# Head products of the state-space stage: four bursts behind units three to six become two bursts behind units four and six

## What is computed

```python
CB = jnp.einsum('bcqgn,bckgn->bcgqk', Cc, Bc)
Lmat = jnp.exp(jnp.where(mask, diff, -jnp.inf))
y_diag = jnp.einsum('bcgqk,bcgrqk,bckgrp->bcqgrp', CB, Lmat, xdt)
y_off = jnp.einsum('bcqgn,bcgrpn,bcqgr->bcqgrp', Cc, h_starts, jnp.exp(acs))
```

## Time and profile before

| | us |
|---|---|
| median of 3 runs | 1998.27 |
| lowest, highest | 1996.66, 1999.34 |
| the profiled execution | 1996.18 |
| its span, first to last instruction | 1994.4 |

### The profile page before, as it was taken

The page is one execution under the profiler, slowest core; times in us unless marked ns, Lnnn a source line. Parts: engine busy times, 40 slices in busy tenths (PEclk is TensorE's granted clock), DMA queues, the critical chain, the costliest instruction groups (busy, mean ns, idle before and its releaser), DMA issues.

```text
span 1994.4 us, 27925 instructions
## 1 busy us (share of the span) xinstructions
PE 1935.1 (97%) x10573; PEld 1642.1 (82%) x10573; DVE 1212.2 (61%) x1688; ACT 1000.2 (50%) x1465; POOL 100.3 (5%) x117
## 2 busy tenths in 40 slices
PE   5889999999999999999999999999999999999999
PEld 3558888888888888887879998787889999998887
DVE  3335645776557888767776676656555454555554
ACT  5434323344555666654445434466544555656642
POOL 1010000000014324000000000000000000000000
PEclk9999999999999999999999999999999999999999
DMA  9973322357656666758875455444565655555554
GB/s 342 349 240 112 100 71 85 97 167 225 196 160 190 192 174 183 233 176 290 317 241 159 149 149 148 145 119 140 176 192 171 188 160 175 168 164 169 169 185 164
DMA packets 210040, 360.39 MB, mean 181 GB/s; under 512 B 14264, under 2 KB 61776, under 8 KB 209024
## 3 DMA queue, kind: packets, MB, share of 16 engines
q1 hardware_dynamic: 200448, 349.36, 56.4%
q10 hardware_dynamic: 8848, 8.47, 1.9%
q0 software_dynamic: 624, 0.92, 0.2%
HBM read 356.55 MB, written 2.16 MB: 180 GB/s over the span
## 4 chain that ended last, share of the span: by engine, by line
PE 86%; DVE 5%; DMA 4%; ACT 2%; SPq 2%; issue 1%; POOL 1%; ACTq 0%; POOLq 0%; DVEq 0%
PE acc L652 48%; PE acc L639 15%; PE acc L619 10%; DMA raw_first<-in_w_ada 2%; SPq L498 1%; DVE w_lo L1879 1%; PE side L1022 1%; DMA ex_a<-acs_scratch 1%; PE side L897 1%; DVE conv L2046 1%; PE side L714 1%; PE side L792 1%; PE side L889 1%; ACT w_hi L1221 1%; PE side L950 1%
## 5 line engine op out<-in xcount | busy, mean ns | idle before, releaser
L1879 DVE TENSOR_TENSOR w_lo<-raw,w_hi 128x1024 fp32r<-128x1024 f32 (+1 forms) x552 | 674.5, 1228 | 431.0 <-ACT w_hi L1221 424.0
L1221 ACT CAST w_hi<-raw 128x1024 fp32r<-128x1024 f32 (+1 forms) x544 | 559.9, 1034 | 579.7 <-PE acc L652 383.2
L652 PE MATMUL acc<-w_hi,h_hi 128*128 128x512 f32 (+1 forms) x1312 | 525.2, 400 | 5.8 <-DVE w_lo L1879 4.0
L652 PE MATMUL acc<-w_hi,h_lo 128*128 128x512 f32 (+1 forms) x1312 | 509.7, 389 | 0.0
L652 PE MATMUL acc<-w_lo,h_hi 128*128 128x512 f32 (+1 forms) x1312 | 508.3, 387 | 0.0
L652 PEld LDWEIGHTS acc<-w_hi,h_hi 128*128 128x128 f32 x1312 | 247.1, 188 | 58.6 <-issue 6.3
L652 PEld LDWEIGHTS acc<-w_hi,h_lo 128*128 128x128 f32 x1312 | 246.8, 188 | 52.7
L652 PEld LDWEIGHTS acc<-w_lo,h_hi 128*128 128x128 f32 x1312 | 247.5, 189 | 46.6
L639 PE MATMUL acc<-h_hi,w_hi 128*128 128x256 f32 x896 | 258.3, 288 | 6.9 <-DVE w_lo L1879 5.6
L639 PE MATMUL acc<-h_lo,w_hi 128*128 128x256 f32 x896 | 254.4, 284 | 0.0
L639 PE MATMUL acc<-h_hi,w_lo 128*128 128x256 f32 x896 | 254.3, 284 | 0.0
(11 more groups left out here) (398 smaller groups left out, 2047.5 us busy)
## 6 DMA issues: line engine op xcount, KB each, us to landing
raw<-in_w_in SPq DMA_DIRECT2D x184, 512.0 KB, 4.4
raw<-in_w_in_odd SPq DMA_DIRECT2D x128, 512.0 KB, 3.7
raw<-in_w_in_even SPq DMA_DIRECT2D x96, 512.0 KB, 3.7
raw<-in_w_out SPq DMA_DIRECT2D x64, 512.0 KB, 5.4
raw_first<-in_w_ada SPq DMA_DIRECT2D x58, 512.0 KB, 8.8
gate_w<-in_w_ada SPq DMA_DIRECT2D x32, 512.0 KB, 6.5
raw<-in_w_out_even SPq DMA_DIRECT2D x32, 512.0 KB, 4.8
raw<-in_w_out_odd SPq DMA_DIRECT2D x32, 512.0 KB, 3.9
```

What stands on the lines that cost most here:

```text
L652: o = nc.tensor.matmul(ACC[b][:, 0:n], l, r, start=first and kk == 0 and m == 0, stop=last and kk == 1 and m == 2)
L1221: act.copy(WHI[:, u % 4, :, 0:n], RAW[:, u % 4, :, 0:n]).then_inc(hi_ready, 1)
L1879: dve.tensor_tensor(WLO[:, u % 4, :, 0:n], RAW[:, u % 4, :, 0:n], WHI[:, u % 4, :, 0:n].bitcast(F32), ALU.subtract).then_inc(lo_ready, 1)
```

## The change

On PE `ssd_y` of heads 0 and 1 is issued together behind unit 4, and that of heads 2 and 3 together behind unit 6; before, each had a place of its own behind units 3, 4, 5 and 6. On DVE `heads(g, 2)` moves from step 6 to step 7, `heads(g, 3)` from 7 to 8 and `y_sum` from 8 to 10. No instruction of PE, DVE, ACT, POOL or SP is added or removed; ACT, POOL and SP keep their order.

```diff
             def ssd_hooks(g):
-                return {0: lambda: ssd_cb(g), 1: lambda: ssd_off(g, 1), 3: lambda: ssd_y(g, 0), 4: lambda: ssd_y(g, 1),
-                        5: lambda: ssd_y(g, 2), 6: lambda: ssd_y(g, 3)}
+                return {0: lambda: ssd_cb(g), 1: lambda: ssd_off(g, 1), 4: lambda: (ssd_y(g, 0), ssd_y(g, 1)),
+                        6: lambda: (ssd_y(g, 2), ssd_y(g, 3))}
...
             def ssd_mid(g):
                 return {3: lambda: (off_out(g, 0), off_out(g, 1)), 4: H(heads, g, 0), 5: H(heads, g, 1),
-                        6: H(heads, g, 2), 7: H(heads, g, 3), 8: H(y_sum, g)}
+                        7: H(heads, g, 2), 8: H(heads, g, 3), 10: H(y_sum, g)}
```

## The result

The median went from 1997.55 to 2007.69 us, a ratio of 1.0052 with a 95% interval of 1.0040 to 1.0063 (seven runs each). The forecast was 1994.8, with a range of 1992.2 to 1998.9; the time lies above the whole range. The profiled execution of the changed kernel took 2009.64, its span 2007.9; it is compared with the profiled 1996.18 of before.

A forecast was written before the change was run, and what follows sets the result against it. PE was taken to bound the kernel, through its own work and 2.7 us of waits ahead of L880. Waits of 2.7 and merging of 0.8 off a median of 1998.27 gave 1994.8 us, range 1992.2 to 1998.9.

The forecast's parts named there:

- What bounds the kernel: PE, busy 97% of the span; beside its own work, 2.7 us of waits ahead of L880 over seven stretches.
- Part 1, the merging: On PE, bursts of L897 merged into sixteen records save 0.05 us per pair, 16 pairs: 0.8 us.
- Part 2: Unit 4 on PE ends 0.94 us earlier, rows are asked for earlier, waits of L880 go: 2.7 us, bounds 0 and 2.7.
- rival B: Waits of L880 stay because weight loads share bandwidth with the rows; only merging pays: 1997.5 us, chance 0.18.
- The safety: At least one DVE low part falls before POOL's masks: up to 1 us more cover, not counted as gain.
- Part 3: DVE's new order costs nothing: head 3's matrix has 0.65 us to spare, and the slightly later `y_sum` stays hidden.
- Both hide it: POOL's masking until 666.83 and the eviction's wait for unit 7 until 664.9 cover `y_sum` ending near 663.7.
- C: A whole weight load ahead of the rows makes L880 wait in all seven stretches: 2003.8 us, chance 0.07.
- E: Head 3's decay matrix comes late from DVE, PE waits 0.3 us in eight second bursts: 1997.2 us, chance 0.05.

The follow-up runs named there:

- kernel with every stretch at 28.08: The change's PE order with DVE's old order, rows asked for after low part 6, POOL's copies ahead of its masks: 1994.41 against 1997.64 us, ratio 0.9985.
- kernel with few pieces: The changed kernel with row DMAs of groups 1 to 7 filling only 16 of 128 partitions: 2004.58 us in a single execution.

## Why the prediction was wrong, point by point

**What bounds the kernel** was right: the waits of L880, 2.7 us in all, were all there was to gain beside the merging. The kernel with every stretch at 28.08 is 3.3 us of stretches below before; the prediction had 3.5.

**Part 1, the merging,** was right and right in size. A burst of sixteen takes 1.70, and a stretch without waits 28.08 instead of 28.17, which is 0.045 per merged pair where 0.05 was forecast.

**Part 2 failed at "So the chain starts some 0.9 earlier. The wait of 0.82 goes".** The first half holds: 0.97 by the trace. The step from an earlier issue to an earlier landing doesn't. I took 6.96 as the price of the second row DMA wherever it is issued, and it had been read in one order of issue alone: rows and load 10 within 0.01 us, the next load 3.15 behind. With the rows 0.95 ahead of load 10 it takes 8.0, and with load 11 1.13 behind load 10 it takes 9.3 to 9.7. "The bounds are 0 ... and 2.7" was wrong at its lower end for that reason: the rows landed 0.5 to 2.3 us later in their stretch than before (2.5 in the stretch with the lower clock), and nothing in the text excluded it. The list of what each moved step issues was made for ACT and not for SP: that low parts 6 and 7 back to back ask for loads 10 and 11 back to back stood only in rival B, as bandwidth.

The safety that Part 2 counted is real. With the low parts out of POOL's way a pair of masks takes 1.44 and not 3.39. It is why masks that start at +24.1 in the kernel with the sum at step 9 end in a stretch of 28.65, while in the one with PE's table alone masks from +22.7 end in 29.20. The rule of the Trainium skill named there (page "SBUF — State Buffer", practical consequences) agrees also with the kernel with few pieces, where DVE's step with two SBUF inputs took 0.74 for 0.35 beside the masks.

**Part 3 failed at "`y_sum` near 663.7 instead of 663.07" and "Both hide it".** From the stretch's start that is +24.3; it ended at +28.7, 4.4 later. The step assumed that ACT can start the high part of unit 10 once unit 6 ends, so that load 10 has landed. That was true with a load of 4.8 us. With 10.4 ACT stands idle for 6.07, some 4.4 of them behind the end of unit 6:

```profile
668.24 1.05 ACT L1221 CAST w_hi<-raw 128x1024 fp32r<-128x1024 f32 x1 [6.07 <-DMA raw<-in_w_in]
```

Moving `y_sum` from 8 to 10 tied the chain to L880 to a transfer that had been off it. This is the larger part: 8.0 of the 9.4 us go when the sum stands one step earlier.

**The rivals.** B and C named the right meeting, loads of weights with the rows, and gave it 0.25 together; both had the wrong price. They reckoned with shares of bandwidth, at most 1.7 us for one load, and looked only at the rows. C's sign, a wait in all seven stretches, is there, and C came nearest with 2003.8. None of them, nor the sum, had the weight load itself late. E's delay of head 3's matrix didn't come here, but showed in the kernel with few pieces.

**The size in all.** Of 209.27 - 199.90 = 9.4: merging -0.6 (7 x 0.09), the late load through `y_sum` +8.0 (changed kernel less the one with the sum at 9), the rest +2.0: rows that land late against masks that are quicker, and the one stretch of 30.43, which has most of it. About 1.6 us of the whole is the clock: behind the wait of 2.35 us at 673.42 the granted clock stood at 0.54 for 3.58 us, and PE's busy time in that stretch is 29.99 instead of 28.35. Behind the longest wait, 2.51 us at 735.45, it stayed at 1.00, so the wait alone doesn't explain it. In the kernel with the sum at 9 no stretch shows that, so these 1.6 are in the 8.0.

```profile
673.42:677.00 3.58, 3.58 (x9) 2.93 (x10) 1.91 (x1) 1.55 (x3) 3.14 (x4) 0.54 0.53 158
```

**What stays open.** Why a load that is asked for just behind the rows' many pieces is hardly served for 3 us, with the DMA engines mostly idle, these runs don't settle. The Trainium skill, page "DMA: Bandwidth & Descriptors", section "Queues, rings and completion order", has SP's and ACT's queues as rings of the same engines, each engine taking turns between those with work. By that rule the load would be expected to begin beside the rows at once; the trace shows 80 and 22 GB/s instead in the 3.40 us behind its issue, and 19 packets of weights against 245 of rows. That points to something ahead of the engines' turns, but no run here shows what. The number of pieces matters, and the bytes matter in some groups; more than that isn't shown.

In the kernel before, three L880 wait on `grp_bc`. In two of these three stretches the masks start at +22.7, and in the third at +22.1. A stretch with masks at +22.65 and no wait shows what else counts: POOL's copies take 0.40 each there, and 0.86 in group 2, where DVE multiplies by the gate at the same time (L2210):

```profile
638.55 0.40 POOL L2738 COPY grp_bc<-bT 128x256 f32 x1
...
666.21 2.02 DVE L2210 TENSOR_TENSOR t<-t,gate_tmp 128x512 f32 x2
```

Why the rows land at +22.6 in some groups and at +22.0 in others is open.

## What to carry to other kernels

Before counting an earlier issue as an earlier arrival, list for every DMA queue what is issued within some 2 us around it after the change, and take the flight time from rows with that order; where no row has that order, the lower bound is a loss. When a step moves behind another on an in-order engine, follow that other step's inputs down to their DMA, and ask what happens if this is 5 us late (as load 10 was here). And a consumer that is last (L880) should not stand behind work it doesn't need (the masks): this reordering was worth more than the change.

## What the hardware showed

- A 512 KB weight load took 3.7 to 7.4 us when asked for within 0.4 us of the first of two row DMAs of 256 pieces each (the kernels with PE's old table or with the rows held back), and 8.0 to 10.6 us when asked for 0.6 to 1.3 us behind it (all others with full rows). With 32 pieces each it took 3.6 to 4.2; with 256 pieces of a quarter of the bytes 5.1 to 8.4.
- The second row DMA took 6.4 to 8.0 with only that load beside it, asked for at the same time; 7.3 to 9.4 with the load 0.6 to 1.3 us behind the first; and 8.3 to 10.3 with a second load within 2.4 us of it.
- Meanwhile the sixteen DMA engines were busy for 0.27 of the 3.40 us behind the issue, and for 0.08 with short pieces: a low DMA share doesn't mean that a new transfer is served.
- Two masks on POOL took 1.44 us alone and 3.39 beside two low parts of DVE; two copies took 0.40 each, or 0.86 beside DVE's L2210.
